# A two-block transformer kernel: the first modulation as column tiles on TensorE, both latent projections in row panels, and bias rows spread by DMA

## The chip, the core and the metric

The kernel runs on one core of a Trainium2 chip. The metric is the device time of one execution in microseconds, and the number compared is the median of several executions. The core has TensorE (PE in the profile, with PEld for its weight loads), VectorE (DVE), ScalarE (ACT), GpSimd (POOL) and SyncE (SP), and 16 DMA engines that all queues share. All arithmetic is float32.

## What is computed

Two transformer blocks are applied to 256 tokens of width 1024. The part that matters here is the head of the first block:

```
cond = silu(c)                                   # 1024 values
mod  = cond @ w_ada + b_ada                      # w_ada is 1024 x 6144
sh1, sc1, gt1, sh2, sc2, gt2 = split(mod, 6)
h    = rmsnorm(x, g_mix) * (1 + sc1) + sh1       # x is 256 x 1024
proj = h @ w_in                                  # 1024 x 4640
a_qkv, c_q, c_kv, k_r, gate_a, gate_b = split(proj)
```

`a_qkv` goes through a dilated attention with a table of relative position biases (8 heads), `c_q` (768 wide) and `c_kv` (256 wide) are the two latents of a multi-head latent attention, and `k_r` (32 wide) is its rotary key. Gated outputs, an output projection and a SwiGLU layer follow, then a second block with its own projections, four mixers (one with another 4 heads of biases) and a second SwiGLU layer. Neither of these later parts is touched.

## The kernel before

**Two-term products.** A weight panel of up to 1024 columns lands in a ring `raw` of 6 slots. ACT rounds it to `w_hi` (L657), DVE makes the rest `w_lo = raw - w_hi` (L1018), and `product` issues three matmuls, hi by hi, hi by lo, lo by hi (L1530, L1531, L1532). Activations have the same two parts, `h_hi` and `h_lo`. ACT and DVE run the splits ahead of PE by `AHEAD` = 4 panels, at the points where the code calls `split.ahead`. SP issues the loads in one fixed order (L595), each waiting until its ring slot is free. Every engine executes its own instructions strictly in the order in which they are written, with semaphores between the engines.

**The prologue.** SP first loads 16 tiles of `w_ada`, each 128 rows by 1024 columns: 8 for `sh1`, 8 for `sc1`. DVE multiplies each by its scalar of `cond` and adds them up in `acc01` (L1072, L1075), and PE sums the accumulator over the partitions with one-column matmuls (`ada_sum`, L1578). In `ada_sum` the stationary operand is a 128x128 piece and the moving operand is a single column. Meanwhile PE transposes `x` (L1590), ACT copies it out as `xT` (L671) and squares it (L678), and PE makes for each of 12 heads the bias row replicated over 128 partitions (L1646, 384 columns), which ACT copies to `bias` (L702). Then come the sum of squares (L1595), its root (L683), its inverse (L1049), and a spread of the inverse over partitions (L1623). `keep_awake` (L1630) issues matmuls whose results are not used.

**The first products.** DVE makes the modulated `h` from `xT`, in 8 tiles of 128 input rows (L1101, L1097, with ACT L696 for the high part), and PE starts on the projections. The latents are 8 chunks (`cq` 0 to 5, `ckv` 0 and 1). Each chunk is 128 output columns over all 1024 input rows, 24 matmuls of 256 columns into one of two banks, `LIN`; ACT squares and rounds each (L720, L721), DVE makes its low part (L1124). Then follow `kr` (32 columns), four chunks `aq`, four `ak`, the token-major `av`, and the up-projections `uq` and `ukv`. After latent chunk 1 ACT writes the replicated rows to DRAM (`head_rows`, L725, 2304 KB), and after `aq2` it reads them back skewed by partition (L742), which gives each token its own shift of the bias.

**The columns of the load order.** A chunk is loaded as 8 pieces of 128 columns, so in runs of 512 bytes; a tile of `w_ada` is loaded as 128 whole rows of 4 KB.

Of the kernel before, what the change touches and what calls it, by code (L numbers as in the profile page):

```python
# [17 lines left out]
P = 128  # L18
SEQ = 256
TT = SEQ // P  # L20
# [102 lines left out]
def build(nc, I, out):  # L123
# [102 lines left out]
    with ctx:  # L226
# [68 lines left out]
        acc01 = take(2, D)  # L295
# [63 lines left out]
        NRM, NRM2 = ps[7][:, SEQ:512], ps[6][:, 0:SEQ]  # L359
        frow_dram = nc.dram_tensor("head_rows", [P, NB * FW], f32, kind="Internal").ap()  # L360
# [4 lines left out]
        ada_used, cmp_used = sem("ada_used"), sem("cmp_used")  # L365
# [99 lines left out]
        for name, n in (("cq", 6), ("ckv", 2), ("kr", 1), ("aq", 1)):  # L465
            L[name] = [output(name, c) for c in range(n)]
# [17 lines left out]
        L["ffn1"] = [output("ffn1", 0 if j == 0 else 3 * j - 1, ("g_sum", FC + j + 1)) for j in range(FC)]  # L484

# [37 lines left out]
        def ada_acc(g):  # L523

            if g < 2:
                return acc01[:, g, :]
            return {2: sq[:, 0:4, :], 3: sq[:, 4:8, :], 4: sq[:, 0:4, :], 5: aqT}[g].rearrange("p a b -> p (a b)")
# [55 lines left out]
        @block.sync  # L583
        def _(sp):
            def load(n, parts, i=0):
                if n >= RAW:

                    o = n - RAW
                    if panels[o][0]:
                        sp.wait_ge(lo_done, order[o] + 1 + i * 6)  # L590
                    else:
                        sp.wait_ge(*((ada_used, order[o] + 1) if order[o] < ADA else (cmp_used, order[o] + 1 - ADA)))
# [54 lines left out]
        def _(act):  # L647
# [20 lines left out]

            for b in range(4):
                act.wait_ge(s("x_t"), b + 1)  # L670
                line(A(xT[:, 2 * b:2 * b + 2, :].rearrange("p a b -> p (a b)"), ps[b][:, :], ACT.Copy), "x_copied")  # L671
            line.settle()
# [7 lines left out]
            def root(k):  # L680

                act.wait_ge(s("ss_done"), k + 1)
# [5 lines left out]

            def highs(k, shift=None):

                for c in range(KC):
                    act.wait_ge(s("h_ready"), 8 * k + c + 1)
                    if shift is None:
                        line(A(h_hi[:, c, :], sq[:, c, :], ACT.Copy), "h_hi")
                    else:
                        line(A(h_hi[:, c, :], sq[:, c, :], ACT.Identity, bias=mod[:, shift, c:c + 1]), "h_hi")  # L696
# [6 lines left out]
            act.wait_ge(s("const_ready"), 1)  # L703
            root(0)

# [3 lines left out]
            act.wait_ge(s("vb_t"), 1)  # L709
            line(A(vb[:, :], ps[2][:, 0:VB_ROWS], ACT.Copy), "vb_ready")  # L710
            split.ahead(-1)
            highs(0, shift=0)


            act.wait_ge(s("h_lo"), 8)
            for c in range(8):
                l = (L["cq"] + L["ckv"])[c]
                split.ahead(outputs[l])
                await_out(act, l)
                line(A(sq[:, c, :], lin(l), ACT.Square), "lat_sq")  # L720
                line(A(mix_hi[:, c, :], lin(l), ACT.Copy, scale=vcol("g_q_lora", c)), "lat_hi")  # L721
                if c == 1:

                    act.wait_ge(s("frow_copied"), NB)
                    act.dma_start(frow_dram, bias[:, :, :].rearrange("p a b -> p (a b)")).then_inc(s("frow_out"), 16)  # L725
# [4 lines left out]
            for c, l in enumerate(L["aq"] + L["ak"]):  # L730
                split.ahead(outputs[l])
                await_out(act, l)
                line(A((aqT if c < 4 else akT)[:, c % 4, :], lin(l), ACT.Copy), free_name(l))
                if c == 0:
# [3 lines left out]
                if c == 2:  # L738
# [143 lines left out]
            act.wait_ge(s("ss_done"), 3)  # L882
# [127 lines left out]
        def _(dve):  # L1010
# [40 lines left out]
            def total(c, k):  # L1051

                if c >= 1:
                    dve.wait_ge(s("sq_ready"), 8 * k + c + 1)
# [4 lines left out]
            def modulate(g, n=1, tell=None):  # L1059

                dve.wait_ge(s("mod_sum"), g + n)
# [4 lines left out]
            def ada(m):  # L1066
# [6 lines left out]
                else:  # L1073
                    dve.wait_ge(ada_used, m)
# [3 lines left out]
            dve.wait_ge(s("cond_ready"), 1)  # L1078
# [7 lines left out]
            modulate(0, 2)  # L1086
            line(stt(out=gs[:, 0, :], in0=mod[:, 1, :], scalar=1.0, in1=va[:, 48:56], op0=add, op1=mult))
# [19 lines left out]
            dve.wait_ge(s("x_copied"), 4)  # L1107
            line.settle()
            normed(0, gs[:, 0, :], 0)
            split.ahead(-1)  # L1110

# [9 lines left out]
            for c, l in enumerate(L["cq"] + L["ckv"]):  # L1121
                split.ahead(outputs[l])
                dve.wait_ge(s("lat_hi"), c + 1)
                line(stt(out=mix_lo[:, c, :], in0=lin(l), scalar=vcol("g_q_lora", c), in1=mix_hi[:, c, :].bitcast(f32),  # L1124
                         op0=mult, op1=sub), free_name(l))
# [60 lines left out]
            for g in range(N1 + 2):  # L1186
# [5 lines left out]
                if g < N1:  # L1192
                    for m in ADA_JOB[g]:
                        if m == 4 * KC:
                            dve.wait_ge(s("mod_sum"), 3)
# [327 lines left out]
        def _(pe):  # L1523
# [50 lines left out]
            def ada_sum(g):  # L1574

                pe.wait_ge(ada_used, KC * (g + 1))
# [8 lines left out]
            line(T.transpose(ps[5][:, 0:VA_ROWS], va_rows, ident[0:VA_ROWS, 0:VA_ROWS]), "va_t")  # L1585
            arrived(pe, "in_x")
# [11 lines left out]
            def sums(k):  # L1598

                if k == 1:  # L1600

                    for c in range(KC):
                        pe.wait_ge(s("sq_ready"), 8 * k + c + 1)
# [3 lines left out]
                elif k == 2:  # L1607

                    pe.wait_ge(s("g_cols_ready"), 1)
                    for c in range(KC):  # L1610
                        pe.wait_ge(s("sq_ready"), 8 * k + c + 1)
# [3 lines left out]
                else:  # L1615
                    pe.wait_ge(s("tot_ready"), 1 if k == 0 else 2)
# [15 lines left out]
            def factor(k):  # L1632
# [4 lines left out]
                else:  # L1637
                    pe.wait_ge(s("inv_col"), k + 1 if k < 2 else k)
                    line(spread(NRM, inv), "inv_ready")
            pe.wait_ge(s("const_ready"), 1)  # L1640
            arrived(pe, "in_rel")
            pe.wait_ge(s("x_copied"), 4)
            for h in range(NB):
                if h >= 4:
                    pe.wait_ge(s("frow_copied"), h - 3)
                line(T.matmul(ps[h % 4][:, 0:FW], relc[:, h:h + 1].to_broadcast([BUCKETS + 1, P]),  # L1646
                              onehot[:, h // A_HEADS, :], start=True, stop=True), "frow_mm")
            sums(0)

            ada_sum(0)  # L1650
            factor(0)
            arrived(pe, "in_vb")
            pe.wait_ge(s("frow_copied"), NB)
            line(T.transpose(ps[2][:, 0:VB_ROWS], vb_rows[0:VB_ROWS], ident[0:VB_ROWS, 0:VB_ROWS]), "vb_t")
            keep_awake(ps[3], 6)
            ada_sum(1)
            keep_awake(ps[3], 2)
# [29 lines left out]

            for name, kn, n, c0 in (("uq", 6, 384, 0), ("ukv", 2, 512, 6)):
# [316 lines left out]
```

## Time and profile before

| | |
|---|---|
| time, median of 3 runs | 867.61 us (866.95 to 872.02) |
| profiled execution | 869.24 us, its span 867.4 us |
| PE busy | 817.1 us, 94% |
| DVE, ACT, POOL busy | 63%, 52%, 7% |
| mean granted TensorE clock | 0.927 |
| HBM traffic over the span | 173 GB/s |

The span is the time from the first to the last instruction; 1.8 us of the profiled execution lie outside it. "Granted clock" is 1.00 where TensorE has its full 2.4 GHz and 0.50 where it has 1.2 GHz. A busy PE is not a PE at its peak, since a matmul at the lower clock counts as busy for twice as long.

### The profile page before, as it was taken

The numbers are of one execution on the slowest core, as the hardware profiler recorded it, in microseconds if no ns is written. First come the engines' busy times: TensorE is split into PE (matmuls) and PEld (weight loads), VectorE is DVE, ScalarE is ACT, GpSimd is POOL, SyncE is SP. The second block draws the span as 40 slices with busy tenths as digits, with TensorE's granted clock in tenths as the row PEclk, the third lists the DMA queues.
The fourth block names the chain that finished last, engine by engine and source line by source line (L and its number), as shares of the span: only waits on it lengthen the run. The fifth ranks groups of instructions, "written<-read, shape, count | busy, mean of one in ns | idle before, by whom it ended". The sixth has DMA issues, their size and how long they took to land.

```text
span 867.4 us, 14523 instructions
## 1 busy us (share of the span) xinstructions
PE 817.1 (94%) x5302; PEld 733.8 (85%) x5302; DVE 548.1 (63%) x1016; ACT 450.4 (52%) x849; POOL 62.9 (7%) x94
## 2 busy tenths in 40 slices
PE   3979997999899999999999999979889999999998
PEld 2679996889699889999999998958788899999997
DVE  3775434978759686666666675447766766666663
ACT  3455445565563565545454556066644654545552
POOL 7001002000034500000000020000000000000000
PEclk9579998999989799999999899569879999999999
DMA  8789864878639646666657475403205466565731
GB/s 266 248 223 299 262 184 137 246 220 249 209 115 297 188 140 198 195 179 185 191 172 196 97 188 159 128 28 95 74 26 169 131 185 190 173 196 173 203 105 49
DMA packets 194349, 151.07 MB, mean 174 GB/s; under 512 B 13298, under 2 KB 178600, under 8 KB 194176
## 3 DMA queue, kind: packets, MB, share of 16 engines
q1 hardware_dynamic: 188896, 143.61, 56.9%
q10 hardware_dynamic: 3760, 5.87, 1.8%
q0 software_dynamic: 1648, 1.00, 0.6%
q8 instruction: 28, 0.46, 0.2%
q14 instruction: 17, 0.14, 0.0%
HBM read 146.78 MB, written 3.41 MB: 173 GB/s over the span
## 4 chain that ended last, share of the span: by engine, by line
PE 79%; DVE 11%; ACT 5%; DMA 2%; issue 2%; ACTq 0%; DVEq 0%
PE ps L1833 19%; PE ps L1530 13%; PE ps L1531 12%; PE ps L1532 12%; PE ps L1835 10%; DVE w_lo L1018 3%; PE ps L1910 2%; ACT w_hi L657 1%; DMA arena<-in_x 1%; PE ps L1646 1%; PE ps L1768 1%; DVE sq L1101 1%; PE ps L1578 1%; PE ps L1746 1%; DVE sq L1075 1%
## 5 line engine op out<-in xcount | busy, mean ns | idle before, releaser
L1018 DVE TENSOR_TENSOR w_lo<-raw,w_hi 128x1024 fp32r<-128x1024 f32 (+3 forms) x223 | 270.7, 1233 | 104.8 <-ACT w_hi L657 104.5
L1833 PE MATMUL ps<-h,w_hi 128*128 128x512 f32 x704 | 254.0, 400 | 1.3 <-DVE h L1097 1.0
L657 ACT ACTIVATE w_hi<-raw 128x1024 fp32r<-128x1024 f32 (+3 forms) x223 | 227.0, 1038 | 30.8 <-PE ps L1532 9.1
L1835 PE MATMUL ps<-h,w_lo 128*128 128x256 f32 x704 | 199.3, 283 | 0.0
L1833 PEld LDWEIGHTS ps<-h,w_hi 128*128 128x128 f32 x704 | 133.1, 189 | 34.3 <-issue 1.7
L1530 PE MATMUL ps<-h,w_hi 128*128 128x256 f32 (+1 forms) x472 | 140.9, 299 | 6.4 <-DVE h L1097 2.2
L1531 PE MATMUL ps<-h,w_hi 128*128 128x256 f32 (+1 forms) x472 | 136.0, 288 | 0.0
L1532 PE MATMUL ps<-h,w_lo 128*128 128x256 f32 (+1 forms) x472 | 135.9, 288 | 0.0
L1835 PEld LDWEIGHTS ps<-h,w_lo 128*128 128x128 f32 x704 | 133.2, 189 | 0.1
L1530 PEld LDWEIGHTS ps<-h,w_hi 128*128 128x128 f32 (+1 forms) x472 | 92.9, 197 | 12.9 <-issue 10.1
L1530 PE MATMUL ps<-g_hi,w_hi 128*128 128x256 f32 x352 | 98.6, 280 | 0.0
L1531 PE MATMUL ps<-g_lo,w_hi 128*128 128x256 f32 x352 | 98.4, 280 | 0.0
L1532 PE MATMUL ps<-g_hi,w_lo 128*128 128x256 f32 x352 | 98.3, 279 | 0.0
L1531 PEld LDWEIGHTS ps<-h,w_hi 128*128 128x128 f32 (+1 forms) x472 | 93.1, 197 | 0.1
L1532 PEld LDWEIGHTS ps<-h,w_lo 128*128 128x128 f32 (+1 forms) x472 | 92.7, 196 | 0.0
L1530 PEld LDWEIGHTS ps<-g_hi,w_hi 128*128 128x128 f32 x352 | 66.2, 188 | 2.0
L1532 PEld LDWEIGHTS ps<-g_hi,w_lo 128*128 128x128 f32 x352 | 66.1, 188 | 0.0
L1531 PEld LDWEIGHTS ps<-g_lo,w_hi 128*128 128x128 f32 x352 | 66.0, 187 | 0.0
L851 ACT ACTIVATE arena<-ps 128x256 f32<-128x256 f32 x44 | 16.9, 383 | 77.4 <-PE ps L1835 77.4
L861 ACT ACTIVATE g_hi<-arena 128x256 fp32r<-128x256 f32 x44 | 18.4, 417 | 45.4 <-DVE arena L1266 45.4
L857 ACT ACTIVATE arena<-ps 128x256 f32<-128x256 f32 x44 | 16.9, 383 | 47.9 <-PE ps L1835 47.9
L1259 DVE TENSOR_TENSOR arena<-arena,ps 128x256 f32<-128x256 f32 x44 | 18.5, 421 | 36.5 <-ACT arena L851 36.5
(325 smaller groups left out, 1177.2 us busy)
## 6 DMA issues: line engine op xcount, KB each, us to landing
raw<-in_w_in SPq DMA_DIRECT2D x53, 512.0 KB, 5.1
raw<-in_w_ada SPq DMA_DIRECT2D x48, 512.0 KB, 4.6
raw<-in_w_down SPq DMA_DIRECT2D x44, 512.0 KB, 4.2
raw<-in_w_gate_up SPq DMA_DIRECT2D x44, 512.0 KB, 4.0
raw<-in_w_gate SPq DMA_DIRECT2D x22, 512.0 KB, 3.9
raw<-in_w_up SPq DMA_DIRECT2D x22, 512.0 KB, 5.0
raw<-in_w_o SPq DMA_DIRECT2D x8, 512.0 KB, 4.8
raw<-in_w_out SPq DMA_DIRECT2D x8, 512.0 KB, 3.6
```

Of the source, the lines that this page charges most:

```text
L657: A(w_hi[:, m % HL, 0:w], raw[:, n % RAW, 0:w], ACT.Copy).then_inc(hi_done, 1)
L851: line(A(g_part[:, j % 2, :], bank_of(f, j)[:, SEQ:512], ACT.Copy), "g_part")
L857: line(A(u_part[:, j % 2, :], UP[j % 2][:, SEQ:512], ACT.Copy), "u_part")
L861: line(A(g_hi[:, j % 2, :], hf[:, j % 2, :], ACT.Copy), "g_hi")
L1018: V.tensor_tensor(w_lo[:, m % HL, 0:w], raw[:, n % RAW, 0:w], w_hi[:, m % HL, 0:w].bitcast(f32), sub).then_inc(lo_done, 1)
L1259: line(V.tensor_tensor(g_all[:, j % 2, :], g_part[:, j % 2, :], bank_of(f, j)[:, 0:SEQ], add), "g_sum")
L1530: T.matmul(dst, stat[0], mov[0], start=start, stop=False, **kw)
L1531: T.matmul(dst, stat[0], mov[1], start=False, stop=False, **kw)
L1532: return T.matmul(dst, stat[1], mov[0], start=False, stop=stop, **kw)
L1833: T.matmul(bank[:, :], hi, h2[:, k, :, :].rearrange("p a b -> p (a b)"), start=(k == 0), stop=False, skip_group_check=True)
L1835: ins = T.matmul(bank[:, 0:SEQ], lo, h_hi[:, k, :], start=False, stop=(k == KC - 1), skip_group_check=True)
L1910: last = T.matmul(ps[7][:, 16 * kv:16 * kv + NCMP], raw[:, n % RAW, k * P:(k + 1) * P], xb[:, kv, 8 * half + k, :], start=(half == 0 and k ...
```

## The change

Three things are changed, all ahead of the chunk `aq0`:

- **Modulation.** The 16 tiles of `w_ada` are now column tiles: all 1024 input rows by 128 output columns. `mod_tile` multiplies one tile by `cond` with 8 accumulating one-column matmuls, straight from `raw`, without a hi/lo split. Tile k of `sc1` (GAIN) and of `sh1` (SHIFT) give what `h` needs for its tile k. DVE adds the bias (`gain_tile`, `shift_tile`).
- **Latents.** They are no longer 8 chunks of output columns but 8 row panels `lat0` to `lat7`: panel k is the 128 input rows of tile k by all 1024 output columns. All 8 outputs accumulate side by side in four banks (`lat`), and the 24 matmuls of panel k need only tile k of `h`. The high and low parts of the latents are now made while `kr`, `aq` and `ak` run.
- **Bias rows.** The 12 rows are made once, without replication, by two matmuls, copied, written to DRAM as `head_row`, and replicated from there to `head_rows` by a DMA between two DRAM tensors.

The sum of squares of `x` is now made by ACT on the token-major `x_tm` with an accumulating Square, before the transposed copies. The two `keep_awake` calls of the prologue are gone. In the core of the diff, lines that only rename or renumber semaphores are left out.

```diff
-    for m in range(ADA_FIRST):
-        ada(m, -1)
-    for c in range(6):
-        chunk("cq", w_in, C_CQ + c * P)
-    for c in range(2):
-        chunk("ckv", w_in, C_KV + c * P)
+    def ada_tile(g, k):
+        directs.append((len(splits) - 1, [(0, KC, P, 0, P, cols(I["w_ada"], g * D + k * P, P))]))
+    for k in range(KC):
+        ada_tile(1, k)
+        panel("lat%d" % k, [(0, 1, D, 0, D, cols(w_in, C_CQ, D, k, 1))])
+        ada_tile(0, k)
...
+        GAIN, SHIFT = ps[4][:, 0:KC], ps[5][:, 0:KC]
...
# ACT
-            for c in range(KC):
-                square(c)
-            for h in range(NB):
-                act.wait_ge(s("frow_mm"), h + 1)
-                line(A(bias[:, h, :], ps[h % 4][:, 0:FW], ACT.Copy), "frow_copied")
...
+            for c in range(KC):
+                act.wait_ge(s("shift_ready"), c + 1)
+                high(0, c, shift=0)
+                split.ahead(min(c + 2, KC - 1) - AHEAD)
             act.wait_ge(s("arg_ready"), 1)
             line(A(sinT[:, :, :], ang, ACT.Sin))
             line(A(cosT[:, :, :], arg, ACT.Sin, scale=-1.0, bias=hpi_c), "trig_ready")
...
+            act.wait_ge(s("frow_copied"), 1)
+            act.dma_start(rows_dram[0:A_HEADS, :], bias[0:A_HEADS, 0, :]).then_inc(s("row_out"), 16)
+            act.dma_start(rows_dram[A_HEADS:NB, :], bias[0:NSA_HEADS, 1, :]).then_inc(s("row_out"), 16)
+            split.ahead(nth("kr") - 2)
+            def latent_high(n):
+                c = LAT_ORDER[n]
+                act.wait_ge(panel_used, nth("lat%d" % (KC - 1)) + 1)
+                if n >= 4:
+                    act.wait_ge(s("lat_lo"), n - 3)
+                line(A(sq[:, c, :], lat(c), ACT.Square), "lat_sq")
+                line(A(mix_hi[:, c, :], lat(c), ACT.Copy, scale=vcol("g_q_lora", c)), "lat_hi")
+            latent_high(0)
+            act.wait_ge(s("row_out"), 32)
+            act.dma_start(frow_dram, bass.AP(rows_dram.tensor, 0, [[0, P], [1, NB * FW]])).then_inc(s("frow_out"), 16)
...
# DVE
-            for m in range(2 * KC):
-                ada(m)
-                if m < KC:
-                    total(m, 0)
-                if m == KC:
-                    inverse(0)
...
+            split.ahead(-AHEAD)
+            for k in range(2):
+                gain_tile(k)
+                shift_tile(k)
+            split.ahead(1 - AHEAD)
+            inverse(0)
+            dve.wait_ge(s("x_copied"), 4)
+            dve.wait_ge(s("inv_ready"), 1)
+            for k in range(KC):
+                line.settle()
+                line(stt(out=sq[:, k, :], in0=xT[:, k, :], scalar=gs[:, 0, k:k + 1], in1=NRM, op0=mult, op1=mult), "h_ready")
+                if k + 2 < KC:
+                    gain_tile(k + 2)
+                dve.wait_ge(s("h_hi"), k + 1)
+                line.settle()
+                line(stt(out=h_lo[:, k, :], in0=sq[:, k, :], scalar=mod[:, 0, k:k + 1], in1=h_hi[:, k, :].bitcast(f32),
+                         op0=add, op1=sub), "h_lo")
+                if k + 2 < KC:
+                    split.ahead(k + 2 - AHEAD)
+                    shift_tile(k + 2)
...
# PE
+            def mod_tile(out_, m, k, told):
+                n = direct_of[m]
+                pe.wait_ge(raw_in[n % RAW], raw_count[n])
+                if k >= 1:
+                    pe.wait_ge(s(told), k)
+                for x in range(KC):
+                    ins = T.matmul(out_[:, k:k + 1], raw[:, n % RAW, x * P:(x + 1) * P], cond[:, x:x + 1],
+                                   start=(x == 0), stop=(x == KC - 1))
+                ins.then_inc(mod_used, 1)
...
-            for l in L["cq"] + L["ckv"]:
-                chunk_out(l, hx, fresh=("h_lo", 0) if l == L["cq"][0] else None)
+            for k in range(KC):
+                if k + 2 < KC:
+                    mod_tile(GAIN, 2 * k + 4, k + 2, "gain_ready")
+                if k == 0:
+                    pe.wait_ge(s("frow_copied"), 1)
+                    pe.wait_ge(s("vb_ready"), 1)
+                m = nth("lat%d" % k)
+                await_split(m)
+                pe.wait_ge(s("h_lo"), k + 1)
+                for n in range(KC):
+                    ins = product(lat(n), hi_lo(m, n * P, P), hx(k), k == 0 and n % 2 == 0, k == KC - 1, shared=True)
+                ins.then_inc(panel_used, 1)
+                if k + 2 < KC:
+                    mod_tile(SHIFT, 2 * k + 5, k + 2, "shift_ready")
```

On PE, from the program's start to the first product, these instructions stand in a row before; L1646 makes the 12 replicated bias rows, L1578 is `ada_sum`, L1630 with `ones,ident` 256 wide is `keep_awake`, and L1530 is the first product:

```order
L1585 MATMUL ps<-ident,arena 128x64
L1590 MATMUL ps<-ident,arena 128x128 x16
L1646 MATMUL ps<-arena 128x384 x12
L1595 MATMUL ps<-ones,tot 128x1 x2
L1578 MATMUL ps<-ones,arena 128x1 x8
L1623 MATMUL ps<-ident,small 128x128 x2
L1654 MATMUL ps<-ident,arena 128x107
L1630 MATMUL ps<-ones,ident 128x256 x6
L1578 MATMUL ps<-ones,arena 128x1 x8
L1630 MATMUL ps<-ones,ident 128x256 x2
L1530 MATMUL ps<-h,w_hi 128x256
```

In the changed kernel the same stretch of PE reads as follows; L1635 is `mod_tile` (8 to a tile), L1645 are the transposes of `x`, L1678 the spread, and L1701 and L1702 the bias rows:

```order
L1626 MATMUL ps<-ident,arena 128x64
L1635 MATMUL ps<-cond,raw 128x1 x16
L1645 MATMUL ps<-ident,arena 128x128 x16
L1635 MATMUL ps<-cond,raw 128x1 x16
L1678 MATMUL ps<-ident,small 128x128 x2
L1701 MATMUL ps<-arena 8x384
L1702 MATMUL ps<-arena 4x384
L1704 MATMUL ps<-ident,arena 128x107
L1635 MATMUL ps<-cond,raw 128x1 x8
L1571 MATMUL ps<-h,w_hi 128x256
```

Five mod tiles now stand ahead of the first product, two of them ahead of the transposes, and the replicated rows and the filler matmuls are gone. Behind the first product the loop repeats 24 product matmuls and a pair of mod tiles; one such boundary on PE is this:

```order
L1573 MATMUL ps<-h,w_lo 128x256
L1635 MATMUL ps<-cond,raw 128x1 x16
L1571 MATMUL ps<-h,w_hi 128x256
```

The x16 are SHIFT of one tile and GAIN of the next; before, nothing stood between the products of the latents. On DVE the chunk of the program that feeds those products was this before, L1072 and L1075 being the sums over `w_ada` and L1101 and L1097 the tiles of `h`:

```order
L1072 TENSOR_SCALAR arena<-raw,cond 128x1024
L1049 RECIPROCAL small<-small 128x2
L1075 SCALAR_TENSOR_TENSOR arena<-raw,cond,arena 128x1024 x7
L1018 TENSOR_TENSOR w_lo<-raw,w_hi 128x1024
L1062 TENSOR_TENSOR mod<-ps,va 128x16
L1087 SCALAR_TENSOR_TENSOR gs<-mod,va 128x8
L1101 SCALAR_TENSOR_TENSOR sq<-xT,gs,ps 128x256 x3
```

Now DVE's order there is the following, where L1103 and L1105 are `gain_tile`, L1109 is `shift_tile`, L1122 the scaled tile and L1127 its low part:

```order
L1072 RECIPROCAL small<-small 128x2
L1122 SCALAR_TENSOR_TENSOR sq<-xT,gs,ps 128x256
L1103 TENSOR_TENSOR mod<-ps,va 128x1
L1105 SCALAR_TENSOR_TENSOR gs<-mod,va 128x1
L1127 SCALAR_TENSOR_TENSOR h<-sq,mod,h 128x256
L1041 TENSOR_TENSOR w_lo<-raw,w_hi 128x1024
L1109 TENSOR_TENSOR mod<-ps,va 128x1
L1122 SCALAR_TENSOR_TENSOR sq<-xT,gs,ps 128x256
```

The 16 sums over 1024 columns are gone from DVE. The `gain_tile` of tile k+2 now stands ahead of the low part of tile k, for which PE's product k waits.

## Rows read from the trace of the kernel before

**Rows 1.** The page: busy tenths of PE and its clock in 40 slices

```profile
PE   3979997999899999999999999979889999999998
...
PEclk9579998999989799999999899569879999999999
```

**Rows 2.** The chain that ended last, first 56 us: start us, us, what

```profile
2.60 11.54 DMA arena<-in_x
...
14.19 3.69 PE ps L1590 x16
...
21.52 10.47 PE ps L1646 x16
...
41.55 7.31 DMA raw<-in_w_in
```

**Rows 3.** Stretches of the prologue: us, busy PE PEld DVE ACT POOL, clock, DMA share, GB/s

```profile
21.80:42.00 20.20, 20.20 (x52) 13.95 (x52) 14.63 (x18) 8.24 (x17) 0.00 (x0) 0.50 0.75 244
45.80:55.60 9.80, 7.57 (x27) 6.39 (x28) 6.84 (x19) 5.86 (x10) 0.00 (x0) 0.50 0.70 183
55.90:78.30 22.40, 21.01 (x176) 20.62 (x176) 15.17 (x22) 12.09 (x22) 0.00 (x0) 1.00 0.99 294
```

**Rows 4.** Timeline of PE: start us, us, line, op; a 128x1 matmul has two records

```profile
36.20 1.20 PE L1623 MATMUL ps<-ident,small 128*128 128x128 f32 x4
...
51.00 0.55 PE L1530 MATMUL ps<-h,w_hi 128*128 128x256 f32 x1 [2.23 <-DVE h L1097]
...
78.12 0.28 PE L1530 MATMUL ps<-h,w_hi 128*32 128x256 f32 x1
```

**Rows 5.** Timeline of PE: `ada_sum` at either clock, and the products' spacing

```profile
179.88 1.95 PE L1578 MATMUL ps<-ones,sq 128*128 128x1 f32 x16
181.69 0.47 PE L1730 MATMUL ps<-qkb 96*128 96x128 f32 x2
...
184.44 0.41 PE L1531 MATMUL ps<-h,w_hi 128*128 128x256 f32 x1
184.66 0.41 PE L1532 MATMUL ps<-h,w_lo 128*128 128x256 f32 x1
...
237.59 3.58 PE L1578 MATMUL ps<-ones,sq 128*128 128x1 f32 x16
241.09 1.11 PE L1768 MATMUL ps<-ptb,arena 128*64 128x256 f32 x2
```

**Rows 6.** Timeline of ACT and DVE: `cond`, the small steps, the pace of `ak` chunks

```profile
9.94 0.21 ACT L667 ACTIVATE cond<-va 128x8 f32<-128x8 f32 x1
...
46.89 0.17 DVE L1062 TENSOR_TENSOR mod<-ps,va 128x16 f32<-128x16 f32 x1 [1.45 <-PE ps L1578]
47.10 0.17 DVE L1087 SCALAR_TENSOR_TENSOR gs<-mod,va 128x8 f32<-128x8 f32 x1
...
50.37 0.48 DVE L1097 SCALAR_TENSOR_TENSOR h<-sq,mod,h 128x256 fp32r<-128x256 f32 x1 [1.73 <-ACT h L696]
...
95.45 0.38 ACT L733 ACTIVATE arena<-ps 128x256 f32<-128x256 f32 x1 [1.39 <-PE ps L1532]
98.17 0.38 ACT L733 ACTIVATE arena<-ps 128x256 f32<-128x256 f32 x1 [1.39 <-PE ps L1532]
```

**Rows 7.** The page's costliest groups: the split of a panel on DVE

```profile
L1018 DVE TENSOR_TENSOR w_lo<-raw,w_hi 128x1024 fp32r<-128x1024 f32 (+3 forms) x223 | 270.7, 1233 | 104.8 <-ACT w_hi L657 104.5
```

**Rows 8.** Stretches with one-column matmuls and behind them: us, PE busy, granted clock, DMA, GB/s

```profile
179.90:181.80 1.90, 1.90 (x18) 1.00 0.88 245
...
182.20:185.50 3.30, 3.30 (x15) 0.50 0.66 194
...
294.90:305.00 10.10, 9.11 (x29) 0.50 0.17 46
...
115.50:119.00 3.50, 3.50 (x34) 1.00 0.02 5
```

**Rows 9.** DMA issues, 55 to 130 us: KB each, us to landing

```profile
head_rows<-bias ACTq DMA_DIRECT2D x1, 2304.0 KB, 10.1
```

More of the change, by code:

```diff
@@ L464, in build @@
         L = {}
-        for name, n in (("cq", 6), ("ckv", 2), ("kr", 1), ("aq", 1)):
+        for name, n in (("kr", 1), ("aq", 1)):
             L[name] = [output(name, c) for c in range(n)]
@@ L667, in _ @@
             line(A(cond[:, :], va[:, 56:64], ACT.Silu), "cond_ready")
+            split.ahead(-AHEAD)
+            arrived(act, "in_x")
+            for t in range(TT):
+                line(A(sq[:, 4 * t:4 * t + 4, :].rearrange("p a b -> p (a b)"), x_tm[:, t, :], ACT.Square,
+                       accum_out=small[:, 68 + t:69 + t]))
+            act.wait_ge(s("const_ready"), 1)
+            line.settle()
+            line(A(rms, small[:, 68:70], ACT.Sqrt, scale=1.0 / D, bias=eps_c), "rms_ready")
             for b in range(4):
@@ L1073, in ada, with gain_tile, shift_tile @@
                 else:
-                    dve.wait_ge(ada_used, m)
+                    dve.wait_ge(ada_used, m - ADA_FIRST)
                     ins = stt(out=acc, in0=w, scalar=cond[:, k:k + 1], in1=acc, op0=mult, op1=add)
                 ins.then_inc(ada_used, 1)
-            dve.wait_ge(s("cond_ready"), 1)
-            for m in range(2 * KC):
-                ada(m)
-                if m < KC:
-                    total(m, 0)
-                if m == KC:
-                    inverse(0)
-            split.ahead(-AHEAD)
-            modulate(0, 2)
-            line(stt(out=gs[:, 0, :], in0=mod[:, 1, :], scalar=1.0, in1=va[:, 48:56], op0=add, op1=mult))
+            def gain_tile(k):
+                dve.wait_ge(mod_used, 2 * k + 1)
+                line(V.tensor_tensor(mod[:, 1, k:k + 1], GAIN[:, k:k + 1], va[:, KC + k:KC + k + 1], add), "gain_ready")
+                line.settle()
+                line(stt(out=gs[:, 0, k:k + 1], in0=mod[:, 1, k:k + 1], scalar=1.0, in1=va[:, 48 + k:49 + k], op0=add, op1=mult))
+            def shift_tile(k):
+                dve.wait_ge(mod_used, 2 * k + 2)
+                line(V.tensor_tensor(mod[:, 0, k:k + 1], SHIFT[:, k:k + 1], va[:, k:k + 1], add), "shift_ready")
+            dve.wait_ge(s("va_ready"), 1)
+            split.ahead(-AHEAD)
+            for k in range(2):
+                gain_tile(k)
+                shift_tile(k)
+            split.ahead(1 - AHEAD)
+            inverse(0)
+            dve.wait_ge(s("x_copied"), 4)
+            dve.wait_ge(s("inv_ready"), 1)
+            for k in range(KC):
+                line.settle()
+                line(stt(out=sq[:, k, :], in0=xT[:, k, :], scalar=gs[:, 0, k:k + 1], in1=NRM, op0=mult, op1=mult), "h_ready")
+                if k + 2 < KC:
+                    gain_tile(k + 2)
+                dve.wait_ge(s("h_hi"), k + 1)
+                line.settle()
+                line(stt(out=h_lo[:, k, :], in0=sq[:, k, :], scalar=mod[:, 0, k:k + 1], in1=h_hi[:, k, :].bitcast(f32),
[3 more added lines that the diff above has]
+                    shift_tile(k + 2)
             def normed(k, gain, shift=None):
@@ L1119, in _ @@
             line(stt(out=spt[5], in0=lam, scalar=-1.0, in1=lam, op0=mult, op1=ALU.max), "lam_abs")
-            for c, l in enumerate(L["cq"] + L["ckv"]):
+            split.ahead(nth("kr") - 2)
+            for n, l in enumerate(L["kr"] + L["aq"] + L["ak"][0:3]):
+                c = LAT_ORDER[n]
                 split.ahead(outputs[l])
-                dve.wait_ge(s("lat_hi"), c + 1)
-                line(stt(out=mix_lo[:, c, :], in0=lin(l), scalar=vcol("g_q_lora", c), in1=mix_hi[:, c, :].bitcast(f32),
-                         op0=mult, op1=sub), free_name(l))
+                dve.wait_ge(s("lat_hi"), n + 1)
+                line(stt(out=mix_lo[:, c, :], in0=lat(c), scalar=vcol("g_q_lora", c), in1=mix_hi[:, c, :].bitcast(f32),
+                         op0=mult, op1=sub), "lat_lo")
             split.ahead(nth("av", 3))
@@ L1585, in _ @@
             line(T.transpose(ps[5][:, 0:VA_ROWS], va_rows, ident[0:VA_ROWS, 0:VA_ROWS]), "va_t")
+            pe.wait_ge(s("cond_ready"), 1)
+            def mod_tile(out_, m, k, told):
[7 more added lines that the diff above has]
+                ins.then_inc(mod_used, 1)
+            mod_tile(GAIN, 0, 0, "gain_ready")
+            mod_tile(SHIFT, 1, 0, "shift_ready")
             arrived(pe, "in_x")
@@ L1639, in factor @@
                     line(spread(NRM, inv), "inv_ready")
+            mod_tile(GAIN, 2, 1, "gain_ready")
+            mod_tile(SHIFT, 3, 1, "shift_ready")
+            factor(0)
             pe.wait_ge(s("const_ready"), 1)
@@ L1642, in _ @@
             pe.wait_ge(s("x_copied"), 4)
[L1643 to L1651, printed above, removed]
+            T.matmul(ps[0][0:A_HEADS, 0:FW], relc[:, 0:A_HEADS], onehot[:, 0, :], start=True, stop=True).then_inc(s("frow_mm"), 1)
+            T.matmul(ps[1][0:NSA_HEADS, 0:FW], relc[:, A_HEADS:NB], onehot[:, 1, :], start=True, stop=True).then_inc(s("frow_mm"), 1)
             arrived(pe, "in_vb")
-            pe.wait_ge(s("frow_copied"), NB)
             line(T.transpose(ps[2][:, 0:VB_ROWS], vb_rows[0:VB_ROWS], ident[0:VB_ROWS, 0:VB_ROWS]), "vb_t")
-            keep_awake(ps[3], 6)
-            ada_sum(1)
-            keep_awake(ps[3], 2)
-            for l in L["cq"] + L["ckv"]:
-                chunk_out(l, hx, fresh=("h_lo", 0) if l == L["cq"][0] else None)
+            for k in range(KC):
[12 more added lines that the diff above has]
+                    mod_tile(SHIFT, 2 * k + 5, k + 2, "shift_ready")
             m, l = nth("kr"), L["kr"][0]
```

74 lines of the change are left out of this document (33 added, 41 removed).

## The prediction

> **What bounds the kernel now.** I read the page first: PE is busy nine tenths of nearly every slice, and its clock is at full in most of them; the two weak places at the start are the first slices, where the clock falls to about half [rows 1]. Next the chain that ended last, for the first 56 us: `x` lands at 14.14, is transposed, then PE makes the replicated bias rows for 10.5 us, and the last long piece is a wait for a weight load [rows 2]. Then the stretches: from 21.8 to 42.0 and from 45.8 to 55.6 the clock is 0.50, and from 55.9 on it is 1.00 with PE busy 21.0 of 22.4 us [rows 3]. Two moments frame the change: the first product starts at 51.00 and the first matmul of `kr` at 78.12, so the 8 latents take 27.1 us [rows 4]. Behind `kr` the `ak` chunks follow each other every 2.72 us, which is PE's own pace (24 matmuls at 0.113) [rows 6]. Everything behind `kr` is the same work in both kernels, so the question is when `kr` starts in the changed one.
>
> **Prices.** A mod tile is the same thing as one `ada_sum`: 8 one-column matmuls with 128x128 float32 weights, two records each. From its start to the next instruction's start it takes 181.69 - 179.88 = 1.8 us at clock 1.00 and 241.09 - 237.59 = 3.5 us at 0.50 [rows 5]. A latent panel has 24 matmuls like a chunk: 2.7 us fast [rows 6], and at the low clock 24 x 0.22 (184.66 - 184.44) = 5.3 us [rows 5]. The old way cost PE two such sums; the new one costs it 16, so 14 more, 25 us at the high clock or 49 at the low. What is taken off PE is 12 replicated rows at 10.47/8 = 1.31 us, less the two that stay: 13 us.
>
> **The start, up to the first product.** PE's order now puts two mod tiles ahead of the transposes and two behind. `cond` is ready at 9.94 + 0.21 = 10.15 [rows 6]. At the low clock: two tiles 7.0 us (17.2), during which `x` lands; transposes 3.7 (20.9) [rows 2]; two tiles (27.9). The inverse of the norm stands on DVE behind the second `shift_tile` and the split of panel 1, so add 0.17 [rows 6], a split of 1.23 [rows 7] and a small step, 1.8 with handoffs (29.7). Then the spread 1.2 (30.9) [rows 4], two bias rows 2.6 (33.5), the small transpose some 0.4, a third of the spread (33.9), and the third GAIN tile 3.5 (37.4). DVE's two small steps of that tile and the low part of `h`, 0.17 + 0.17 + 0.48 [rows 6], make 1.2 with handoffs: the first product starts at 38.6. At the high clock the same list gives 14.19 + 3.7 for the transposes, 3.6, 1.8, 0.6, 1.3, 0.2, 1.8 and 1.2 = 28.4. I take 38.0, near the slow end, because PE did short work here before too and was at 0.50 from 21.8 on [rows 3]. The tiles' landing costs nothing as far as I can see: SHIFT of tile 0 is third in SP's order and has till 13.7. So the first product is 13 us **earlier** than the 51.00 of before. DVE's sums over `w_ada` and the squares of `xT` went off the path; that is the gain of the change.
>
> **The latents.** Before, eight dense chunks follow. Now each period is product, SHIFT(k+2), GAIN(k+3), and a wait: product k+1 needs DVE's `gain_tile` and then the low part of `h`, both behind the GAIN tile just done, 1.2 us that nothing on PE covers. DVE's split (1.23) and ACT's high part lie beside the mod tiles and cost nothing. At the high clock a period is 2.7 + 1.8 + 1.8 + 1.2 = 7.5 us, at the low one 5.3 + 3.5 + 3.5 + 1.2 = 13.5.
>
> Which clock? [...] After the 1.9 us of `ada_sum` at 179.9 the clock is 0.50 for 3.3 us though PE had no idle time (busy 1.90 of 1.90, then 3.30 of 3.30); behind other such sums, from 294.9 on, it is 0.50 for 10 us; but 3.5 us of one-column sums at 115.5, with dense products on both sides, left it at 1.00 [rows 8]. Here 3.6 us of them plus 1.2 us idle follow each 2.7 us of products, twice as much as at 179.9. One low stretch of 3.3 us takes 1.65 us of work's worth, two take 3.3: a period of 9.2 to 10.8. I take 10.5, nearer to two because the sparse part is longer than the one in either row that lost the clock.
>
> The Trainium skill ("TensorE: Matmul & The Clock Gate", section "Why this matters for your kernels") asks only that there be no PE-idle gaps of more than about 3 us between matmul bursts. By that rule the loop would keep the high clock, since its longest idle piece is 1.2 us; the row at 182.2 speaks against the rule, as PE had not been idle at all before it.
>
> Five such periods are 52.5 us. The tail is product 5, SHIFT 7, a wait of 1.9 (shift, scale 0.48, high part on ACT about 0.5, low part 0.48, handoffs), products 6 and 7: 11.9 fast, 21.3 slow, 15 taken. So `kr` starts at 38.0 + 52.5 + 15 = **105.5**, against 78.1: 27.4 us later.
>
> **What is left.** DMA: before, the stretch 55.9 to 78.3 moved 294 GB/s [rows 3], in runs of 512 bytes; the loop needs 3 tiles of 0.524 MB per 10.5 us, 150 GB/s, and each is asked for two periods ahead. No cost. The panels of `kr` and `aq` are then all loaded. On ACT, behind the last high part, stand now a sine pair with its table load, two small DMA issues, three splits, a latent eviction and a wait for the small DMAs; the eviction of `kr` and `aq0` come late. The `aq` chunks start from the 2 us that this pile exceeds `kr`'s 2.7: I estimate 1.5 us, with 0 and 3 as bounds. The replication between DRAM tensors has the 2304 KB of the write that it replaces, which took 10.1 us [rows 9], and ACT waits for it only five chunks (some 16 us) later; no cost at up to 1.5 times that price. In the later stages nothing moves.
>
> Sum: 27.4 + 1.5 = +29. Against the profiled execution, span 867.4 + 29 = 896.4 and 898.2 with the 1.8 outside it; that execution lay 1.6 above the median, so the median becomes 867.6 + 29 = **896**.
>
> **Rivals.**
> - *The clock stays up in the loop, after a slow start.* This is what the page's rule gives: 38.6 + 5 x 7.5 + 11.9 = 88.0, +9.9 and 1.5: 879. For it: the 3.5 us at 115.5 that cost no clock. Against it: 182.2 and 294.9 [rows 8].
> - *The loop is slow throughout.* 38.6 + 67.5 + 21.3 = 127.4, +49.3 + 1.5: 918. For it: 294.9 to 305.0, 10 us low after sums with PE busy 9.1 of them. Against it: the full products of 5.3 us at the low clock should bring it back, as they did at 55.6, 4.6 us after the first product at 51.0 [rows 3, 4].
> - *Not slower: the high clock from the first mod tile on.* Then the first product is at 28.4, the loop ends at 28.4 + 37.5 + 11.9 = 77.8, and the time is 867 to 869, within 1% of before. It decides at a start of the products under some 30 us together with a period of 7.5; to be faster by 1% it would need the 1.2 us wait of each period hidden as well and the pile on ACT gone. Against it: PE has only short and sparse work until the products, and the clock from 21.8 to 42.0 is 0.50 with PE busy all the time [rows 3].
> - *The replication is late.* If the copy between DRAM tensors takes 25 us instead of 10.1, ACT holds the splits for 8 us or so: 904 on top of the forecast's loop.
>
> **How the numbers follow.** Mixed clock, 885 to 908: 0.57. Slow throughout, about 918: 0.12. High clock in the loop, about 879: 0.15. High clock from the start, 867 to 869: 0.08. Late replication, 904: 0.04. Something better than all of these, under 859: 0.04. The likeliest case gives 896. The range leaves out the last two ends: 876 to 915. A difference under 1% (8.7 us) can't be told from none with this kernel. Slower by over 1%: 0.87; within 1%: 0.09; faster: 0.04.
>
> **What would show it.** In the changed profile: first product near 38; 16 groups of one-column matmuls of 1.8 to 3.5 us on PE; between the pairs and the next product an idle of 1.2 us put down to DVE's low part; granted clock between 0.5 and 1.0 in the loop, changing inside it; first `kr` matmul near 105; DMA share in the loop about half of what it was; the end shifted by the same amount as `kr`, give or take 2. The forecast is wrong if mod tiles cost PE less than 1.8 us, if products start under 30, or if waits for landings of `raw` show up inside the loop.

## The result, and the profile after

The changed kernel takes 893.0 us (median of 4, 886.63 to 895.71) against 867.28 before (median of 4). Over all these executions it takes 1.028 times as long, with a 95% interval of 1.025 to 1.032. The forecast was 896.

The page of the changed kernel, PE and its clock in 40 slices of 22.1 us, answers to [rows 1]:

```profile
PE   5888899799989999999999999979979999999998
...
PEclk9666899999988999999999999879979999999999
```

Where the kernel before had two weak slices, this one has four, slices 2 to 5, with the clock at six or eight tenths. Behind them the two read nearly alike; the largest difference is in slice 26, five tenths before and eight now. The timeline of PE shows what stands there (start us, us, line; L1635 is the mod tile, 16 records each, L1645 the transposes, L1571 a product); it answers to [rows 4, 5]:

```profile
10.84 6.99 PE L1635 MATMUL ps<-cond,raw 128*128 128x1 f32 x32 [1.83 <-ACT cond L676]
17.69 3.64 PE L1645 MATMUL ps<-ident,arena 128*128 128x128 f32 x16
21.13 3.72 PE L1635 MATMUL ps<-cond,raw 128*128 128x1 f32 x32
...
30.36 3.45 PE L1635 MATMUL ps<-cond,raw 128*128 128x1 f32 x16
...
34.95 0.55 PE L1571 MATMUL ps<-h,w_hi 128*128 128x256 f32 x1 [1.14 <-DVE h L1127]
...
39.33 4.69 PE L1635 MATMUL ps<-cond,raw 128*128 128x1 f32 x32
...
49.55 4.67 PE L1635 MATMUL ps<-cond,raw 128*128 128x1 f32 x32
...
102.41 0.28 PE L1571 MATMUL ps<-h,w_hi 128*32 128x256 f32 x1
```

The first product starts at 34.95, 16.0 us earlier than the 51.00 of [rows 4]. The first matmul of `kr` starts at 102.41, 24.3 later than 78.12. The 8 latents take 67.5 us instead of 27.1. A period (39.33 to 49.55) is 10.2 us: the product takes 4.4, the pair of mod tiles 4.6, and the idle time before the next product 1.2. Stretches inside one period and over the whole loop (us, PE busy, granted clock, DMA share, GB/s):

```profile
34.90:39.30 4.40, 4.35 (x24) 0.62 0.84 238
39.30:43.90 4.60, 4.60 (x34) 0.76 0.32 91
43.90:45.10 1.20, 0.12 (x1) 0.50 0.30 89
```

The dense part runs mostly at the low clock and the sparse part mostly at the high one: the clock rises toward the end of the products and falls again inside the mod tiles, in every period. The idle 1.2 us is filled by three small steps on DVE. Ahead of the first product they are these (start us, us, what), which answers to [rows 6]:

```profile
33.85 0.17 DVE mod L1103
34.04 0.17 DVE gs L1105
34.32 0.49 DVE h L1127
```

Past `kr` nothing moved: the last of the eight `aq` and `ak` evictions is at 103.61 before and at 127.92 now, 24.3 apart, the same as `kr`. The profiled execution as a whole is only 17.4 us longer (span 884.8 against 867.4), and the difference is a matter of the clock, whose falls in the later stages differ from execution to execution. The stretch from `kr` to the end, in the profile before and then in the one after:

```profile
78.10:867.40 789.30, 759.15 (x5014) 0.94 0.57 166
```

```profile
102.40:884.80 782.40, 749.09 (x5014) 0.96 0.58 170
```

The same 5014 records took 6.9 us less at 0.96 than at 0.94. The profiled execution, 886.63, was the shortest of the four, which lie 9.1 us apart; the median's shift of 25.7 fits the 24.3 at `kr`. In what follows the start of `kr` is the measure, since everything the edits touch is in front of it. It is known only for the one profiled execution of each kernel.

### The profile page after: what moved, and what is told of

Same layout as the page of the kernel before. It is cut to its first block, busy times and chain, and to the rows that moved or that the text cites. A ratio compares the mean times of both kernels' runs of the same rounds, so it can differ in the third digit from the quotient of the medians.

```text
span 884.8 us, 14891 instructions
## 1 busy us (share of the span) xinstructions
PE 830.8 (94%) x5486; PEld 754.4 (85%) x5486; DVE 531.6 (60%) x1015; ACT 443.9 (50%) x835; POOL 63.1 (7%) x94
## 4 chain that ended last, share of the span: by engine, by line
PE 82%; DVE 11%; ACT 4%; issue 2%; DMA 1%; ACTq 0%; DVEq 0%
PE ps L1892 18%; PE ps L1571 13%; PE ps L1572 12%; PE ps L1573 12%; PE ps L1894 9%; PE ps L1635 4%; DVE w_lo L1041 3%; PE ps L1969 1%; ACT w_hi L666 1%; PE ps L1827 1%; DVE sq L1145 1%; PE ps L1619 1%; PE ps L1805 1%; DVE sq L1098 1%; PE ps L1980 1%
## 5 line engine op out<-in xcount | busy, mean ns | idle before, releaser
L666 ACT ACTIVATE w_hi<-raw 128x1024 fp32r<-128x1024 f32 (+3 forms) x223 | 226.6, 1038 | 22.0 <-PE ps L1573 10.6
L1571 PE MATMUL ps<-h,w_hi 128*128 128x256 f32 (+1 forms) x472 | 142.3, 302 | 12.4 <-DVE h L1127 8.8
L1571 PEld LDWEIGHTS ps<-h,w_hi 128*128 128x128 f32 (+1 forms) x472 | 94.9, 201 | 17.7 <-issue 16.4
L1571 PE MATMUL ps<-g_hi,w_hi 128*128 128x256 f32 x352 | 98.6, 280 | 0.0
L1572 PEld LDWEIGHTS ps<-h,w_hi 128*128 128x128 f32 (+1 forms) x472 | 94.8, 201 | 0.1
L1571 PEld LDWEIGHTS ps<-g_hi,w_hi 128*128 128x128 f32 x352 | 66.2, 188 | 2.1 <-issue 0.2
L874 ACT ACTIVATE arena<-ps 128x256 f32<-128x256 f32 x44 | 16.9, 383 | 77.2 <-PE ps L1894 77.2
L1635 PEld LDWEIGHTS ps<-cond,raw 128*128 128x128 f32 x256 | 39.6, 246 | 2.0 <-ACT cond L676 2.0
L1635 PE MATMUL ps<-cond,raw 128*128 128x1 f32 x256 | 39.2, 287 | 1.8 <-ACT cond L676 1.8
```

The source lines that it names most:

```text
L666: A(w_hi[:, m % HL, 0:w], raw[:, n % RAW, 0:w], ACT.Copy).then_inc(hi_done, 1)
L874: line(A(g_part[:, j % 2, :], bank_of(f, j)[:, SEQ:512], ACT.Copy), "g_part")
L1571: T.matmul(dst, stat[0], mov[0], start=start, stop=False, **kw)
L1572: T.matmul(dst, stat[0], mov[1], start=False, stop=False, **kw)
L1635: ins = T.matmul(out_[:, k:k + 1], raw[:, n % RAW, x * P:(x + 1) * P], cond[:, x:x + 1], start=(x == 0), stop=(x == KC - 1))
```

## The experiments

| run | first product | `kr` | us | against before |
|---|---|---|---|---|
| before | 51.00 | 78.12 | 867.28 | |
| the change | 34.95 | 102.41 | 893.0 | 1.028 (1.025 to 1.032) |
| e1_one_matmul | 26.07 | 72.72 | 862.97 (one) | |
| e2_low_first | 36.85 | 98.23 | 886.97 | 1.021 (1.014 to 1.029) |
| e3_filler | 35.12 | 98.58 | 886.07 (one) | |
| e10_low_filler | 38.55 | 104.90 | 893.37 (one) | |
| e6_mod_first | 74.27 | 98.29 | 888.74 (one) | |
| e4_bias_only | 47.83 | 74.95 | 866.22 | 0.997 (0.994 to 0.999) |
| e5_bias_squares | 41.93 | 69.05 | 858.11 | 0.988 (0.984 to 0.992) |
| e7_panels_dve | 39.66 | 65.33 | 856.59 | 0.986 (0.982 to 0.991) |
| e8_sums_early | 38.96 | 66.09 | 854.10 | 0.983 (0.978 to 0.988) |
| e9_panels_early | 37.74 | 63.41 | 852.40 | 0.982 (0.978 to 0.985) |

A single time is marked (one). The ratios compare with executions of the kernel before that were taken beside each run, with medians of 867.3 to 868.7.

The theory was the prediction's: the mod tiles on PE, their clock and the wait behind them cost more than the earlier start gives. The rivals: the loss lies in the row panels, the loads in column tiles, or the bias rows by DMA.

**The tiles themselves.**

```diff
-                for x in range(KC):
+                for x in range(1):
                     ins = T.matmul(out_[:, k:k + 1], raw[:, n % RAW, x * P:(x + 1) * P], cond[:, x:x + 1],
-                                   start=(x == 0), stop=(x == KC - 1))
+                                   start=True, stop=True)
```

> The changed kernel with one of the 8 matmuls of each mod tile (the other seven are left out, so the modulation is wrong; loads and waits are all there). In the changed kernel the first product starts at 34.95, a period of the loop is 10.2 us and kr starts near 102.4. If the one-column matmuls on TensorE are what the latents pay for, the period falls to some 5 us (2.7 of products, 1.2 of wait, 0.5 of what is left of two mod tiles, and then perhaps the loads, 3 tiles of 0.524 MB at 300 GB/s being 5.2 us), the first product comes before 25, kr starts at 60 to 70, and the time is 850 to 860. If the loop is held by something else (the wait for DVE, the splits, the row panels, the column tiles' loads), kr stays behind 85.

`kr` starts at 72.72, 29.7 us earlier than with all eight matmuls, and the first product at 26.07. So 7/8 of the one-column work carry more than the whole loss of 24.3 us; the loads, the splits, the panels and the bias rows are all still there. The forecast numbers were missed (a first product before 25, `kr` at 60 to 70, 850 to 860 us), since the periods are 6.7 us, not 5. The timeline of PE in this run (x4 are the two single matmuls of a pair of tiles) shows it:

```profile
43.19 0.50 PE L1635 MATMUL ps<-cond,raw 128*128 128x1 f32 x4
49.83 0.50 PE L1635 MATMUL ps<-cond,raw 128*128 128x1 f32 x4
```

With the mod tiles short, DVE's shift, scale and low part and ACT's high part between them, no longer covered by a GAIN tile, keep PE waiting some 1.75 us a period (43.69 to 45.45), and the products, now the only dense work, still run in part at the low clock. The whole stretch from the first product to `kr` (us, PE busy, PEld, DVE, ACT, POOL, clock, DMA share, GB/s):

```profile
26.05:72.70 46.65, 36.05 (x214) 35.74 (x215) 19.36 (x43) 12.53 (x19) 0.00 (x0) 0.76 0.77 215
```

These 46.65 us are still 19.5 more than the 27.1 of before. PE is idle for 10.6 of them, each time until DVE's low part of `h`. So making `h` tile by tile, between products that wait for it, has a price of its own beside the one-column matmuls.

**The wait, and the clock.** In e2 DVE's low part of tile k goes ahead of the next `gain_tile`:

```diff
-                if k + 2 < KC:
-                    gain_tile(k + 2)
                 dve.wait_ge(s("h_hi"), k + 1)
...
                 if k + 2 < KC:
+                    gain_tile(k + 2)
                     split.ahead(k + 2 - AHEAD)
```

> The changed kernel with DVE's low part of h(k) ahead of gain_tile(k+2), so that product k no longer waits for the GAIN tile just done. If the waits add up as in my sum (1.2 us a period, of which some 0.2 stays), the period falls from 10.2 to 9.2 and kr starts 6 to 7 us earlier, near 96. [...]

In e3 two matmuls that nobody needs stand in the wait:

```diff
+                if k + 2 < KC:
+                    keep_awake(ps[6], 2)
                 m = nth("lat%d" % k)
```

> The changed kernel with two unused float32 matmuls of 128x256 in each of the six waits between a GAIN tile and the product behind it (0.9 us together at the high clock, 1.7 at the low). If the clock falls because the loop is thin just there, it stays up longer and the period falls below 9.5, kr near 97. If the one-column matmuls themselves make the thin stretch, the clock falls all the same and kr starts 0 to 3 us later than 102.4.

The loop from first product to `kr` is 67.5 us in the change, 61.4 in e2 and 63.5 in e3. The stretches of the loop, first of the change, then of e2, then of e3 (us, PE busy, PEld, DVE, ACT, POOL, clock, DMA share, GB/s):

```profile
34.95:102.40 67.45, 59.83 (x368) 59.49 (x369) 19.19 (x43) 12.21 (x18) 0.00 (x0) 0.67 0.53 148
```

```profile
36.80:98.20 61.40, 59.13 (x369) 58.96 (x370) 19.76 (x45) 12.21 (x18) 0.00 (x0) 0.72 0.58 162
```

```profile
35.10:98.50 63.40, 60.95 (x390) 58.82 (x389) 18.99 (x43) 12.21 (x18) 0.00 (x0) 0.76 0.57 158
```

In e2 the idle time is nearly gone (7.6 us idle became 2.3) and the loop is 6.1 us shorter: the wait was a real cost of the size forecast, 1 us a period. The clock rises only from 0.67 to 0.72, so it is not the idle time alone that keeps it down. `kr` comes only 4.2 us earlier, because the first product comes 1.9 us later. The pair of mod tiles behind the transposes, which the edit does not touch, took 6.83 us in this execution against 3.72 in the change's:

```profile
21.23 6.83 PE L1634 MATMUL ps<-cond,raw 128*128 128x1 f32 x32
```

In e3 PE does more work and is done 4 us sooner; the clock is 0.76 where it was 0.67. Both edits together:

> The changed kernel with both edits of the loop: DVE's low part ahead of the next gain_tile, and two filler matmuls between each GAIN tile and the product. Each alone brought kr from 102.4 to 98.2 and 98.6. If the wait and the clock were separate costs, kr starts near 94. If the filler earns only by standing in the wait, which is gone here, its own 0.9 to 1.7 us a period are paid and kr starts at 99 to 106.

The second branch came true: `kr` at 104.90, and a loop of 66.4 us from the first product at 38.55. The loop is 5.0 us longer than that of e2, at the same clock of 0.72. So filler paid only while it stood in a wait; with the wait gone it was simply more to do. This rests on one traced execution of each kernel. The four executions of the change lie 9.1 us apart in time and its loop was seen in one of them, so 4.0 us gained and 5.0 us lost are not shown to be clear of that spread. Neither edit, nor both, gets near the 27.1 us of before.

**All mod tiles first.**

```diff
+            for k in range(2, KC):
+                mod_tile(GAIN, 2 * k, k, "gain_ready")
+                mod_tile(SHIFT, 2 * k + 1, k, "shift_ready")
             for k in range(KC):
-                if k + 2 < KC:
-                    mod_tile(GAIN, 2 * k + 4, k + 2, "gain_ready")
...
-                split.ahead(min(c + 2, KC - 1) - AHEAD)
+                split.ahead(min(c + 2, 5) - AHEAD)
```

> The changed kernel with all 16 mod tiles ahead of the first product and the 8 panels' products dense behind them; loads, splits and sums are the same. Twelve tiles at 3.5 us instead of one ahead of the products put the first product at about 69 to 74 (at the high clock, 1.8 each, at 50), and the eight products take about 24 to 27 as they did before (27.1). If the loop's cost is the sum of its parts at a low clock, kr starts at 94 to 100, a little ahead of 102.4, since the 1.2 us waits go and the products run at the high clock after their first 5 us. If the one-column tiles get the high clock when they stand alone, kr starts before 80.

The timeline of PE in this run:

```profile
33.41 40.99 PE L1635 MATMUL ps<-cond,raw 128*128 128x1 f32 x192
74.27 0.56 PE L1571 MATMUL ps<-h,w_hi 128*128 128x256 f32 x1
```

Twelve tiles take 41.0 us without a gap, 3.4 each: the low price of [rows 5]. The 8 products then take 24.0, and `kr` starts at 98.29. This is the change's bill laid out in two items: 41 us of thin work plus 24 of dense. In this execution, as in e2's, the pair behind the transposes took 6.83 us instead of 3.72, so the start of `kr` hides part of the difference. From the start of the third GAIN tile to `kr` it is 64.9 us here (from 33.41) and 72.1 in the change (from 30.36): interleaving cost 7 us more than doing one behind the other.

**What the change gained.** e4 has only the bias rows of the change, e5 the bias rows and ACT's squares of `x`, both on the kernel before:

```diff
-            for h in range(NB):
-                act.wait_ge(s("frow_mm"), h + 1)
-                line(A(bias[:, h, :], ps[h % 4][:, 0:FW], ACT.Copy), "frow_copied")
+            act.wait_ge(s("frow_mm"), 2)
+            line(A(bias[0:A_HEADS, 0, :], ps[0][0:A_HEADS, 0:FW], ACT.Copy))
+            line(A(bias[0:NSA_HEADS, 1, :], ps[1][0:NSA_HEADS, 0:FW], ACT.Copy), "frow_copied")
...
# e5 alone
+            for t in range(TT):
+                line(A(sq[:, 4 * t:4 * t + 4, :].rearrange("p a b -> p (a b)"), x_tm[:, t, :], ACT.Square,
+                       accum_out=small[:, 68 + t:69 + t]))
...
-                if m < KC:
-                    total(m, 0)
```

> The kernel before with the bias rows alone made once and spread by DMA; the squares stay on the transposed x and their sums on DVE. PE loses ten of the twelve matmuls of 1.3 us ahead of the sum of squares, but DVE reaches the end of its own eight partial sums (0.41 us each, among the sums over w_ada) only at 28.9. So the sum of squares starts near 29 instead of 31.9, and kr 3 us earlier, near 75: 864 to 865. If instead the bias rows were the bound of the prologue, this alone gives what the run with both parts gave (kr at 69.05, 9.1 us earlier).

> The kernel before with two parts of the change: the bias rows made once and spread by DMA, and the squares of x summed by ACT on x_tm. The modulation stays on DVE in row tiles, the latents stay 8 dense chunks. If what the change gained lies in these parts and what it lost in the mod tiles on TensorE, DVE runs its 16 sums of 1.3 us without a stop from 14.3 to about 35, the first product starts near 41 instead of 51, kr near 68, and the time is about 857, 1.2% under before. The rival: the loads of w_ada and of the first chunk hold it, the first product stays behind 47, and the time is within 0.5% of before.

Both came out close to the forecast: `kr` 3.2 and 9.1 us earlier, though e4's time, 866.22, is just above 864 to 865. The chain of e4 (start us, us, what) shows DVE's partial sums as the next to be late, then the sum of squares:

```profile
28.95 0.42 DVE tot L1060
...
29.42 1.03 PE ps L1599 x4
```

e7 is the changed kernel with its modulation undone (DVE's sums over row tiles, `ada_sum`, `keep_awake` back), so it differs from e5 in the row panels and what goes with them (ACT takes the latents out, and issues the DMA of `head_rows`, behind the last panel):

> The changed kernel with its modulation undone: DVE's sums over row tiles of w_ada and ada_sum as before, with the row panels of the latents, the bias rows by DMA and ACT's squares of the change kept. If the row panels cost and gain nothing by themselves, it equals the run with bias rows and squares alone (first product 41.9, kr 69.05, 858 us) within 1.5 us. If the panels were a part of the loss (splits that come late, products that wait for h tile by tile), kr starts behind 72. If they gain (no eviction between chunks), before 67.5.

The panels gain: `kr` at 65.33. Of the 3.7 us, 2.3 are before the first product and 1.4 in the latents. The first is a wait for weights. ACT splits four panels or chunks before it makes the high part of `h`, and the chain goes through the load of the fourth, in e5 and then in e7 (chain, start us, us):

```profile
32.44 7.35 DMA raw<-in_w_in
```

```profile
31.68 5.84 DMA raw<-in_w_in
```

The fourth panel, in rows of 4 KB, was there 2.3 us sooner than the fourth chunk in runs of 512 bytes. ACT's four splits, each waiting for its load, start 1.8 us apart in e5 (34.38 to 39.80) and 1.3 apart in e7 (33.70 to 37.55). One issue on SP takes 1.7 us in the median for a chunk and 0.33 for a panel; whether the issue or the length of the runs sets the pace was not tried. The latents then take 25.7 instead of 27.1.

**A version that beats both.** The chain of e5 has a piece of 6.33 us for a load of `w_ada` (18.40 to 24.73). It is no wait of DVE, though the expectation of e8 below takes it for one. The load was asked for when a sum freed its ring slot, and DVE went on with other sums until it landed. The timeline of DVE in e5:

```profile
14.30 9.63 DVE L1080 SCALAR_TENSOR_TENSOR arena<-raw,cond,arena 128x1024 f32<-128x1024 f32 x7
...
24.75 9.62 DVE L1080 SCALAR_TENSOR_TENSOR arena<-raw,cond,arena 128x1024 f32<-128x1024 f32 x7
```

So DVE sums nearly without a stop from 13.4 to 34.4, as the expectation of e5 said. Each ring slot comes free when DVE has worked off its tile, and the loads of the first weights come behind these. The first sum starts only behind the angle steps, at 13.4, and so the slots come free late. e8 is e5 with this edit, e9 is e7 with it:

```diff
                 ada(m)
+                if m == 3:
+                    angles()
```

> The kernel with bias rows by DMA and ACT's squares on the old modulation, and besides DVE's first four sums over w_ada put ahead of its angle steps (which wait for the positions' DMA until 11.4 and run to 13.5). The sums start at 10.2 instead of 13.4 and hand their ring slots back 3 us earlier, so loads and sums end 3 us earlier: first product near 39, kr near 66, 855 us. If the loads' own rate is the bound (the wait of 6.3 us for w_ada at 18.4), the gain is under 1 us.

> The three parts that gained, together: row panels of the latents, bias rows by DMA and ACT's squares, with the modulation on DVE in row tiles and its first four sums ahead of the angle steps. Panels alone put kr at 65.33 and the early sums alone at 66.09, against 69.05 without either. If both gains add (3.7 and 3.0), kr starts at 62.4 and the time is 851 to 853. If both only shorten the same wait for the first weight load, kr starts at 65 and the time is that of the runs with one of them, 854 to 857.

Early sums gave 3.0 us at `kr`. The first sum starts at 10.13 instead of 13.43, but the last ends only 1.5 us earlier (32.89 against 34.37), since the angle steps now stand among them. What counts is the fourth weight load, which is there 3.0 us earlier. With both, `kr` starts at 63.41, between the two forecasts: 5.6 of the 6.7 us add up. What the last one waits for now is DVE, which sums without a stop until PE's `ada_sum` can start (chain of e9):

```profile
31.75 1.29 DVE arena L1094
33.09 2.35 PE ps L1609 x16
35.47 0.19 DVE mod L1081
```

e9 takes 852.4 us, 0.982 of before (0.978 to 0.985): everything of the change but the mod tiles on PE, and DVE's sums started earlier.

## Why the prediction was right

**The start** was forecast at 38.0 and is 34.95. The list of steps is the right one; the price of GAIN and SHIFT of tile 1 was wrong. I charged them 7.0 us at the low clock and they took 3.7 (21.13), at the spacing of the full clock. The other three tiles cost 3.5 each as priced. That the pair was fast is chance: the same instructions in the same place took 3.7 us in e3 and 6.8 in e2, e6 and e10. With 6.8 the start would have been at the forecast 38.0. Which of the two the other three executions of the change had isn't known.

**The period** was forecast at 10.5 (7.5 to 13.5) and is 10.2. Its parts: product 4.4 between 2.7 and 5.3, the pair 4.6 between 3.6 and 7.0, the wait 1.2 as worked out. The reading from [rows 8], that short one-column work behind dense work brings the clock down even while PE is busy, held: five periods, five falls, each inside a pair of mod tiles. e2 supports it, with a clock of 0.72 and hardly any idle time.

**The Trainium skill's rule** ("TensorE: Matmul & The Clock Gate", "Why this matters for your kernels"), no idle gap above some 3 us, would have given 879. The longest idle piece between the first product and `kr` is 1.98 us (ahead of product 6), 1.2 inside a period, and the clock is 0.67 over the stretch, so here keeping to the rule does not keep the clock.

**The tail** was forecast at 15 and is 16.5 (85.91 to 102.41). **The pile on ACT** was forecast at 1.5 us and cost nothing: 24.3 at `kr` and 24.3 at the last eviction of `ak`. The sum was 27.4 us at `kr` and is 24.3: the start came 3.0 us sooner than forecast, and the five periods, 1.5 us shorter, and the tail, 1.5 longer, cancel. With 1.5 for the pile the forecast was +28.9; the median moved by 25.7. Part of the agreement is luck, in the fast pair and in what cancels. One sign was missed: the end was to shift by the same amount as `kr`, give or take 2, and in the profiled execution it shifted by 17.4 against 24.3, because behind `kr` the clock was 0.96 instead of 0.94. A slip in the chances: the cases slower by over 1% add up to 0.88, not 0.87.

**The replication between DRAM tensors** took 12.9 us against 10.1 of [rows 9] and stayed covered, as forecast; it was issued at 102.6 and awaited at 122.6:

```profile
head_rows<-head_row ACTq DMA_DIRECT2D x1, 2304.0 KB, 12.9
```

**What I had not priced** is the gain of the parts by themselves. I called DVE's relief "the gain of the change" and gave it 13 us at the first product. There the bias rows and squares alone give 9.1 and the panels 2.3 more (e7, 39.66), and the move to PE gives the other 4.7 of the measured 16.0. e9, without the move, has its first product at 37.74, so most of this gain did not need it.

## What to carry to other kernels

A matrix-vector product as one-column matmuls makes PE load every weight for a single column: 1.8 us per 128 x 1024 piece of float32 at the high clock, 3.4 at the low, against 1.3 us for one sum on DVE (16 of them ran from 13.4 to 34.4 in e5). Price it by weight loads, and price the dense work around it at a lower clock too: over the latents the granted clock was 0.67 here. And look at what must happen between a thin piece and the dense piece that waits for it, since that chain comes once a period. When a change has several parts, run each part alone before judging the whole: here the whole lost 2.8%, while two of its parts without the third gained 1.4%, and 1.8% with DVE's sums started earlier. Where a wait is next to dense work, take the wait away rather than fill it: here that gave 6.1 us of the loop, filling it gave 4.0, and doing both gave 1.1 (one traced execution of each).

## What the runs showed that was not expected

- The clock printed for the first stretch is not always one that PE had. In e6 the stretch 33.4 to 74.2 reads 1.00, and yet its 192 records take 0.2135 us each, the spacing of the low clock, and the products behind them are 0.21 apart until 77.2:

```profile
33.40:74.20 40.80, 40.80 (x193) 1.00 0.58 162
```

The view appears to show 1.00 as long as no change of the clock has been recorded; the spacing of matmuls is the safer reading.
- The periods of the change are alike to 0.05 us (39.33, 49.55, 59.78, 69.96, 80.18), with the fall of the clock at the same place in each. In e3 the starts of the pairs are 7.7, 9.2, 10.5 and 10.4 us apart. Why the unfilled loop settles into one period was not tried.
